# A two-layer encoder trunk on one core: engine loops written out, and the modulation products of the second FFN moved into its first up tiles

## The reference, cut to what matters

```python
for l in range(DEPTH):                                   # DEPTH = 2, SEQ = 512, D_MODEL = 1024, D_FF = 2816
    mod = jax.nn.silu(c) @ mod_w[l] + mod_b[l]           # 1024 x 9216: nine parts of 1024
    sh1, sc1, g1, sh2, sc2, g2, sh3, sc3, g3 = jnp.split(mod, N_MOD, axis=-1)
    h = modulate(rms_norm(x, norm_g[l, 0]), sh1, sc1)
    x = x + 0.5 * g1[:, None, :] * swiglu(h, ffn1_w1[l], ffn1_w3[l], ffn1_w2[l])
    h = modulate(rms_norm(x, norm_g[l, 1]), sh2, sc2)
    x = x + g2[:, None, :] * hybrid_mixer(h, ...)        # top-k attention beside a state-space scan, GLU, w_out
    h = modulate(rms_norm(x, norm_g[l, 2]), sh3, sc3)
    x = x + 0.5 * g3[:, None, :] * swiglu(h, ffn2_w1[l], ffn2_w3[l], ffn2_w2[l])
return rms_norm(x, final_g)
# swiglu(h, w1, w3, w2) = (silu(h @ w1) * (h @ w3)) @ w2
```

## Time and profile before

| | us |
|---|---|
| median of 3 runs (range) | 2422.61 (2420.08 to 2428.3) |
| span of the profiled execution | 2414.7 |
| PE busy | 2225.4 (92%) |
| PE weight loads busy | 1753.0 (73%) |
| DVE busy | 1175.1 (49%) |
| ACT busy | 720.1 (30%) |
| POOL busy | 232.5 (10%) |

### The profile page before, as it was taken

The page is one execution under the profiler, slowest core; times in us unless marked ns, Lnnn a source line. Parts: engine busy times, 40 slices in busy tenths (PEclk is TensorE's granted clock), DMA queues, the critical chain, the costliest instruction groups (busy, mean ns, idle before and its releaser), DMA issues.

```text
span 2414.7 us, 29806 instructions
## 1 busy us (share of the span) xinstructions
PE 2225.4 (92%) x9837; PEld 1753.0 (73%) x9837; DVE 1175.1 (49%) x1869; ACT 720.1 (30%) x1094; POOL 232.5 (10%) x463
## 2 busy tenths in 40 slices
PE   3999999788888899999989999988788988999998
PEld 3888878556666678887878888866556666888886
DVE  7654534554663443344465554445556344333544
ACT  2322222322223253332233222222222334333222
POOL 0000000092410000000000000005434000000000
PEclk9999999986566899999989999999855689999998
DMA  7556533311000233345455564332100012333542
GB/s 269 183 176 198 173 104 99 76 36 44 7 6 18 71 86 88 104 144 171 156 165 185 182 185 142 93 90 62 49 6 6 6 57 82 87 104 122 183 151 84
DMA packets 378189, 256.63 MB, mean 106 GB/s; under 512 B 37744, under 2 KB 356824, under 8 KB 378072
## 3 DMA queue, kind: packets, MB, share of 16 engines
q1 hardware_dynamic: 365256, 250.45, 34.6%
q10 hardware_dynamic: 12816, 4.76, 1.1%
HBM read 250.72 MB, written 2.10 MB: 105 GB/s over the span
## 4 chain that ended last, share of the span: by engine, by line
issue 73%; PE 19%; DVE 5%; ACT 2%; ACTq 1%; DMA 0%; POOL 0%; DVEq 0%; POOLq 0%
PE ps L1717 3%; PE ps L1469 2%; PE ps L1668 2%; PE ps L1470 2%; PE ps L1471 2%; PE ps L1715 2%; PE ps L1643 1%; PE ps L1624 1%; PE ps L1634 1%; ACTq L721 1%; PE ps L1608 1%; PE ps L1616 1%; ACT tmp_b L567 1%; PE ps L1686 1%; DVE score L1177 1%
## 5 line engine op out<-in xcount | busy, mean ns | idle before, releaser
L1469 PE MATMUL ps<-h_hi,w_hi 128*128 128x512 f32 x1760 | 706.1, 401 | 37.6 <-DVE h_lo L896 20.8
L1470 PE MATMUL ps<-h_lo,w_hi 128*128 128x512 f32 x1760 | 693.4, 394 | 0.0
L1471 PE MATMUL ps<-h_hi,w_lo 128*128 128x512 f32 x1760 | 692.5, 393 | 0.0
L847 DVE TENSOR_TENSOR w_lo<-stage,w_hi 128x1024 fp32r<-128x1024 f32 (+2 forms) x322 | 375.5, 1194 | 237.2 <-ACT w_hi L547 226.8
L1469 PEld LDWEIGHTS ps<-h_hi,w_hi 128*128 128x128 f32 x1760 | 335.9, 191 | 130.5 <-issue 40.5
L1470 PEld LDWEIGHTS ps<-h_lo,w_hi 128*128 128x128 f32 x1760 | 336.1, 191 | 71.1 <-issue 3.5
L1471 PEld LDWEIGHTS ps<-h_hi,w_lo 128*128 128x128 f32 x1760 | 335.2, 190 | 71.2
L547 ACT ACTIVATE w_hi<-stage 128x1024 fp32r<-128x1024 f32 (+2 forms) x322 | 315.7, 1016 | 102.7 <-PE ps L1471 99.5
L1469 PE MATMUL ps<-g_hi,w_hi 128*128 128x512 f32 x704 | 282.4, 401 | 5.1 <-DVE g_lo L1083 5.1
L1470 PE MATMUL ps<-g_lo,w_hi 128*128 128x512 f32 x704 | 281.9, 400 | 0.0
L1471 PE MATMUL ps<-g_hi,w_lo 128*128 128x512 f32 x704 | 281.5, 400 | 0.0
(11 more groups left out here) (265 smaller groups left out, 1976.4 us busy)
## 6 DMA issues: line engine op xcount, KB each, us to landing
stage<-in_ffn_w SPq DMA_DIRECT2D x242, 512.0 KB, 4.8
mod_stage<-in_mod_w SPq DMA_DIRECT2D x144, 512.0 KB, 6.1
stage<-in_ffn_w SPq DMA_DIRECT2D x32, 384.0 KB, 5.1
stage<-in_w_in SPq DMA_DIRECT2D x20, 512.0 KB, 3.8
mod_first<-in_mod_w SPq DMA_DIRECT2D x4, 2048.0 KB, 21.6
stage<-in_w_out SPq DMA_DIRECT2D x16, 512.0 KB, 3.8
x_in<-in_x SPq DMA_DIRECT2D x1, 2048.0 KB, 10.4
stage<-in_w_in SPq DMA_DIRECT2D x8, 256.0 KB, 3.5
```

Of the source, the lines that this page charges most:

```text
L847: V.tensor_tensor(w_lo[:, c % RING, 0:n], stage[:, c % RING, 0:n], w_hi[:, c % RING, 0:n].bitcast(F32), ALU.subtract).then_inc(w_split_lo. ...
L1469: mm(out, hi, rhs_hi, start=first, stop=False)
L1470: mm(out, hi, rhs_lo, start=False, stop=False)
L1471: return mm(out, lo, rhs_hi, start=False, stop=last)
```

## The change

- `Fori(0, DEPTH)` becomes a Python loop on all engines, and the up tiles of both FFNs are written out. Every wait compares with a constant (`Signal.at`), and all addresses are constants.
- The second FFN makes its three parts in up tiles 0 to 11, two chunks per tile, with `mod_sum` and `mod_out` after tiles 4, 8 and 12.
- In the first FFN the `mod_sum` of part 7 moves from behind the last up tile to behind the first down tile. The other five stay where they were.

```diff
-A_UNROLL = 4
-A_TURNS = (FT - 2) // A_UNROLL
-MOD_TURN = ((0, 1, 2), (3, 4, 5), (6, 7), ())
-MOD_REST = ((0, 1, 2, 3, 4), (5, 6, 7))
+MOD_CHUNKS = (
+    [[KT * (f // 4) + i for i in ((0, 1, 2), (3, 4, 5), (6, 7), ())[f % 4]] for f in range(20)] +
+    [list(range(5 * KT, 5 * KT + 5)), list(range(5 * KT + 5, 6 * KT))],
+    [[6 * KT + 2 * f, 6 * KT + 2 * f + 1] if f < 12 else [] for f in range(FT)])
+MOD_SUM = ({4 * j + 3: j for j in range(5)} | {FT: 5}, {4: 6, 8: 7, 12: 8})
...
+    def at(self, layer, k):
+
+        return self.sem, self.after(layer, k)
...
 # SP
-                    with sp.Fori(0, A_TURNS) as i:
-                        for u in range(A_UNROLL):
-                            load_up(l, ffn, A_UNROLL * i + (u + 1), c0 + 2 * (u + 1), shift=2 * A_UNROLL * i)
...
+                    for f in range(FT):
                         c = c0 + 2 * (f + 1)
...
+                        for q in MOD_CHUNKS[ffn][f]:
+                            load_mod(l, q)
...
-                        if ffn == 1:
-                            for q in (2 * n, 2 * n + 1):
-                                load_mod(l, q0 + KT + q, (l + 1) % DEPTH, q // KT)
...
 # DVE
+                for f in range(FT):
                     for j in range(2):
                         split_lo(l, c0 + 2 * (f + 1) + j)
+                    for q in MOD_CHUNKS[ffn][f]:
+                        mod_chunk(l, q)
+                    dve.wait_ge(*silu_done.at(l, f0 + f))
+                    dve.wait_ge(*g_done.at(l, f0 + f - 2))
+                    V.tensor_tensor(tmp_b[:, f % 2, :], tmp_a[:, f % 2, :], ps[:, 2 * (f % 2) + 1, :], ALU.mult).then_inc(g_full.sem, 1)
+                    dve.wait_ge(*g_hi_done.at(l, f0 + f))
+                    V.tensor_tensor(g_lo[:, f, :], tmp_b[:, f % 2, :], g_hi[:, f, :].bitcast(F32), ALU.subtract).then_inc(g_done.sem, 1)
+                    if f in MOD_SUM[ffn]:
+                        mod_out(l, MOD_SUM[ffn][f])
...
 # PE
-                for f in (FT - 2, FT - 1):
-                    tile_pe(l, ffn, f, f % 2, 0, 0, False)
-                mod_sum(l, A_TURNS + ffn)
-                wait(pe, g_done, l, f0 + FT - 1)
+                for f in range(FT):
+                    tile_pe(l, ffn, f)
+                    if f in MOD_SUM[ffn]:
+                        mod_sum(l, MOD_SUM[ffn][f])
+                pe.wait_ge(*g_done.at(l, f0 + FT - 1))
...
-                        if ffn == 1 and n % 4 == 3:
-                            mod_sum(l, A_TURNS + 2 + n // 4)
+                        if FT + n in MOD_SUM[ffn]:
+                            mod_sum(l, MOD_SUM[ffn][FT + n])
...
-            with pe.Fori(0, DEPTH) as l:
+            for l in range(DEPTH):
```

More of the change, by code:

```diff
@@ L421, in load_w, with load_mod @@
                     sp.dma_start(dst[:, :, t, :], v).then_inc(w_loaded[c % RING], 16)
-            def load_mod(layer, q, src_layer, part, shift=0):
-                sp.wait_ge(m_used.sem, m_used.after(layer, q - MOD_RING) + shift)
+            def load_mod(layer, q):
+                src_layer, part = mod_of(layer, q // KT)
+                sp.wait_ge(*m_used.at(layer, q - MOD_RING))
                 src = a["mod_w"].rearrange("l k n -> (l k) n")[
@@ L541, in _, with split_hi @@
         def _(act):
[L542 to L546, removed]
+            def split_hi(layer, c):
+                n = chunk_size(c)
+                act.wait_ge(w_loaded[c % RING], slot_loaded(layer, c))
+                used(act, layer, c - RING)
                 nc.scalar.activation(w_hi[:, c % RING, 0:n], stage[:, c % RING, 0:n], ACT.Copy).then_inc(w_split_hi.sem, 1)
@@ L817, in mixer_act @@
                     squares(l, KT + n)
-            with act.Fori(0, DEPTH) as l:
+            for l in range(DEPTH):
                 norm_hi(l, 0, 0)
@@ L866, in mod_chunk, with mod_out @@
                 i.then_inc(m_used.sem, 1)
-            def mod_out(layer, j, part, bias_layer, turn=0):
-                dve.wait_ge(mod_psum.sem, mod_psum.after(layer, j) + turn)
-                V.tensor_tensor(modc[:, ds(part, 1), :].rearrange("p a k -> p (a k)") if not isinstance(part, int) else modc[:, part, :],
-                                ps[:, 7, 0:KT], modb[:, ds(bias_layer * (N_MOD * KT) + part * KT, KT)],
+                if k == KT - 1:
+                    dve.wait_ge(*m_used.at(layer, q))
+                    V.memset(s5_t[:, 13, 0:1], 0.0).then_inc(acc_ready.sem, 1)
+            def mod_out(layer, j):
+                bias_layer, part = mod_of(layer, j) if j >= 0 else (layer, j + 2)
+                dve.wait_ge(*mod_psum.at(layer, j))
+                V.tensor_tensor(modc[:, part, :], ps[:, 7, 0:KT], modb[:, ds(bias_layer * (N_MOD * KT) + part * KT, KT)],
                                 ALU.add).then_inc(mod_done.sem, 1)
@@ L1085, in ffn_dve @@
-                settle(dve)
-                with dve.Fori(0, A_TURNS) as i:
-                    for u in range(A_UNROLL):
-                        for j in range(2):
-                            split_lo(l, c0 + 2 * (u + 1) + j, shift=2 * A_UNROLL * i)
-                        if ffn == 0:
-                            for q in MOD_TURN[u]:
-                                mod_chunk(l, q, shift=KT * i, turn=i)
-                                if q == KT - 1:
-                                    acc_done(l, KT - 1, 0, shift=KT * i)
-                        product(u, u % 2, A_UNROLL * i)
-                        product_lo(u, u % 2, A_UNROLL * i)
-                    if ffn == 0:
-                        mod_out(l, 0, i + 2, l, turn=i)
@@ L1342, in _ @@
             steps = [0]
-            with dve.Fori(0, DEPTH) as l:
+            for l in range(DEPTH):
                 steps[0] = 0
@@ L1380, in power @@
             def power(layer, idx):
-                wait(pool, ms_ready, layer, idx)
+                pool.wait_ge(*ms_ready.at(layer, idx))
                 Q.tensor_tensor(rstd[:], ms[:], mhalf[:], ALU.pow).then_inc(rstd_ready.sem, 1)
@@ L1432, in _ @@
             pool.wait_ge(credits, 3)
-            with pool.Fori(0, DEPTH) as l:
+            for l in range(DEPTH):
                 step = Chain(pool, pool_step, l, POOL_STEPS)
@@ L1488, in feature_sums @@
             def feature_sums(layer, k3):
-                wait(pe, sq_sum, layer, (k3 + 1) * (KT - 1) - 1)
+                pe.wait_ge(*sq_sum.at(layer, (k3 + 1) * (KT - 1) - 1))
                 for b in range(QB):
@@ L1495, in squares_sum @@
             def squares_sum(layer, e, buf, done, src, last_k, k):
-                wait(pe, done, layer, e)
+                pe.wait_ge(*done.at(layer, e))
                 for b in range(QB):
```

388 lines of the change are left out of this document (168 added, 220 removed).

## The result

| | before | after |
|---|---|---|
| median of 20 runs (range), us | 2421.72 (2414.16 to 2428.3) | 2427.64 (2423.09 to 2428.85) |
| span of the profiled execution, us | 2414.7 | 2426.0 |

The ratio of the times is 1.0021, with a 95% interval from 1.0013 to 1.0029: 5.9 us slower by the medians, inside the 0.3% that I had called no change. The two profiles differ by 11.4 us. They aren't equally typical. The device time is about 1.8 us above the span in nearly every run here, so before's profile shows an execution of some 2416.5 us, and only 2 of the 20 runs of before are as short as that or nearly (2414.16 and 2416.78). After's profile (2427.83 us) is in the middle of its runs.

A forecast was written before the change was run, and what follows sets the result against it. PE was taken to bound the FFN up tiles, short waits between engines to count in the mixer if on the path. 10.8 - 0.4 - 1.9 - 1.9 - 4 = +2.6 us on the 2422.6 median gave 2425 us; 8-in-10 range 2409 to 2436.

The forecast's parts named there:

- step 5: Mixer: masks wait 0.22 us instead of 0.38 without register instructions, half assumed on the path; -4 us (0 to -10).
- Sums: Six sums leave gaps or stretches where they cost PE nothing for full stretches, 1.80 us each; +10.8 us.
- Gap: Ahead of the down tiles: 0.1 us of PE register instructions gone, four times; -0.4 us (0 to -0.9).
- Table loads: Second FFN's first up tile: without ACT's 1.28 us load, PE starts tile 1 earlier; -1.9 us, 1.1 and 0.8 by layer.
- Ends of the layers: Last down matmul to norm end: mod_out and DVE's loop jump no longer delay feature sums; -1.9 us, 1.5 and 0.4.
- 6. and 7.: Loop edges, code size and modulation loads cost nothing; new chunk wait after up tiles 4 and 8 has 3.8 us slack.
- rival C: Loop edges cost more than PE shows: 0.44 us back in each of 20 turns, -8.8; 2416 us; chance 8%.
- Rival A: Bare gaps ahead of down tiles bring one more half-clock stretch each, 6.4 us in all; 2436 us; chance 16%.
- Rival B: Mixer gives more: step 5's full bound plus better clock, or the same by clock alone; 2410 us; chance 20%.
- D: New chunk wait in second FFN's up tiles bites: PE loses 2 us at four places, +8; 2433 us; chance 6%.

The follow-up runs named there:

- sums back: Changed kernel with modulation chunks and sums where the kernel before has them, the rest still written out; 2415.2 us, 0.9969 of before.
- last parts left out: Changed kernel with before's sum places, the layer's last mod_out behind the squares, and the last layer's two unused modulation parts dropped; 2412.64 us, 0.9939 of before.
- DVE's loop: Changed kernel with the two layers as a loop again on DVE alone; 2425.46 us, 1.0011 of before.
- five matmuls: Changed kernel with five extra unused matmuls on PE ahead of up tile 1 of the second FFN; 2427.32 us, 1.0020 of before.
- table load back: Changed kernel with a one-column Exp on ACT at the second FFN's start, forcing a table load; 2420.13 us, 0.9983 of before.
- two accumulators: Kernel without the last layer's unused modulation parts, now alternating two accumulators so sums can wait for gaps; 2406.89 us, 0.9917 of before.

## Why the prediction was right, and where it wasn't

The forecast was 2425, the time 2427.64; the move, +2.6 forecast, was +5.9. Outside the mixers I had forecast +6.6 us, and the two profiles give +6.1. That is better than my terms deserve: 1.6 us more at the norms ahead of the mixers, which I hadn't seen, is paid for by gains that came out larger than in my terms or weren't in them at all. That they cancel is luck. The miss is step 5.

I had taken the 7.9 us between span and median for time outside the span. It is 1.8 us of that; the rest is that the profile showed a short execution.

1. **Sums.** Right in size: 1.85, 1.64 and 1.77 us per sum in a full stretch (sums back, last parts left out). Three net per layer, 3 x 1.8 x 2 = 10.8. My sign of it, 248.4 us for the second FFN's up tiles, counted a sum twice: the 244.1 that I started from ran to the end of part 8's sum, one of the three that I added. From 242.39 it is 242.4 + 5.4 - 1.1 = 246.7, and 246.94 and 246.68 were measured.
2. **Gap.** 2.97 to 2.80 us, four times: -0.7 for the -0.4 taken, within its bounds.
3. **Table loads.** The up tiles grew by 4.55 and 4.29 us where three sums cost about 5.5: -1.0 and -1.2, for -1.1 and -0.8 forecast. The load put back by itself costs 1.0 and 1.26.
4. **Ends of the layers.** -1.6 and -0.7, for -1.5 and -0.4. But I hadn't seen that the half clock would only move: with the sum in the first FFN's down tiles, their feature sums took 1.87 us (438.49:449.99 at 0.60), and the norm ahead of each mixer grew by 0.8, +1.6 in all. The sum there need not be the cause: this norm took 11.5 us in one pass of before too, and 10.7 in one pass each of the kernels with DVE's loop and with the five matmuls, which have the sum in the down tiles.
5. **Mixer.** The step that failed. The masks' hop did shrink from 0.38 to 0.22 us, as said. Nothing of the 4 us came. The masks' idle time fell by 2.5 us in both layers together, half of what the hops gave back, and the mixers didn't follow. With DVE's registers back the hop was 0.38 again and no mixer was longer. At equal clock there is nothing either: three mixers of before with 211.7 to 212.6 us at the low level took 388.97 to 389.73 us, the changed kernel's second, with 212.5, took 389.81. So the share on the path, which I had taken as a half, is none that these runs can see. Which engine the masks wait for instead is less sure than the rows look: between the profiles with and without DVE's loop the label moves from PE (85.7 to 65.1) to ACT (16.3) with little change in the sum (95.6 to 96.8).
6. and 7. **Nothing.** PE was busy 246.93 of 246.94 us in the second FFN's up tiles, with no idle time behind tiles 4 and 8; the first FFN's took 250.8 and 250.6 us, before 251.3 and 250.8. That is 0.6 and 0.2 us less, where rival C needed 2.2 each, so it is out. My sign for it, up tiles of the first FFN under 252 us, was no sign: the 253.01 that I compared with ended with part 7's sum, which the change takes out, so it would have come true in any case. No up tile here shows PE waiting at a loop edge.

Without the mixers the measured terms, with 0.3 us less in the two norms ahead of the second FFN and 0.7 less in the first FFN's up tiles, give 10.8 - 0.7 - 2.2 - 2.3 + 1.6 - 0.3 - 0.7 = +6.2, against +5.9 by the medians. For the mixers that leaves about nothing, and a spread that is larger: the six mixers of before average 388.4 us, the two of the changed kernel 389.6.

**Rival A** was wrong as I put it: behind the bare gaps there is one stretch of 3.41 us as before, not two. It had a grain in it: in the three written-out kernels with before's place of the sums the low level didn't come behind the second FFN's gap at all, and the changed kernel has it there, for 1.3 to 1.5 us in each layer. But it stayed behind the first FFN's gap with the sum in it, and with the table load back it was gone from a bare gap. Where the gap falls against the 3.41 us steps fits all of these, with or without the sum; why it does, no run here shows. **Rival B** (a mixer 10 us shorter) and **D** didn't come.

The changed kernel lost, then, because its two halves pull apart: written out with the sums left in the gaps is 0.9969 of before; the move of the sums costs 12.4 us by the medians (10.8 for the sums, about 3 for the half clock behind the second FFN's gaps and 1.6 at the norms, both as the stages happened to fall, 2.2 given back at the two layer ends: 13.2) and turns that into 1.0021.

## What to carry to other kernels

In this kernel a sum of 1.8 us in a gap of the engine that bounds was free, and the same sum between full tiles cost all of it; before work is moved to smooth another engine's load, look where it stood on the bounding one. Removing register instructions from an engine pays only where a wait behind them is on the path; ask first what the waiting engine will wait for instead. Where one stage varies by 9 us from run to run of the same program, compare stage by stage, and read a small change of the whole from medians.

## What I hadn't expected of the hardware

- The same mixer took 384.44 to 393.21 us in six passes of an unchanged program, at mean granted clocks of 0.75 to 0.72.
- Behind gaps of about 3 us in which a full stretch was ended, the clock was at 0.50 for 3.41 us, for twice that in some passes (down tiles 126.66 for 125.5 us), or not at all (the second FFN's gaps of four kernels, eight of eight; three have the sum in the gap, one hasn't; and two of the four gaps with two accumulators). Each such stretch costs 1.2 to 2 us. Which of the three it is went by where the gap began within the clock's 3.41 us steps, in all 53 gaps of 2.8 to 3.0 us.
- A kernel with one more table load on ACT per layer, 1.28 us that nobody needs, had 0.9983 of before's time where the one without had 1.0021. The gain lies in stretches at half clock that fell otherwise. Such a gain is not a reason to keep the work.
